# Hybrid attention, pooling, Fourier and mixture-of-experts backbone: branch projections as three products of split weights, and an opening in another order

## The chip, the cores and the metric

The kernel runs on one core of a Trainium2 chip. The metric is the device time of one execution in microseconds (us). Inputs are rearranged on the host beforehand and do not count.

## What is computed

Two layers run over 512 tokens of width 1024: 256 context tokens and 256 latent ones. The last layer needs context tokens as keys and values alone. Cut to what matters here:

```
for layer in range(2):
    h = rmsnorm(x, g_norm1) * (1 + scale1) + shift1       # shift, scale: c @ w_mod + b_mod
    p = h @ w_in                                           # q, kv, rope, pool, fourier, 3 gates
    a = attention(p)    # 8 heads, keys of context and latent tokens
    b = pooling(p)      # 4 window sizes, then a 128x128 product per group, times s_pool
    c = fourier(p)      # 2-D, per group of 128 channels
    g = sigmoid(p_gates + b_gate)
    y = g[0] * (a @ w_oa) + g[1] * (b @ w_ob) + g[2] * (c @ w_oc)    # branch projections
    x = x + gate1 * (y @ w_out)
    h = rmsnorm(x, g_norm2) * (1 + scale2) + shift2
    x = x + gate2 * (swiglu(h) if layer == 0 else top-2-of-8 experts(h))
return rmsnorm(x, g_final)
```

Everything is float32. Most products are made in a reduced format from two parts: a weight w is split into hi (w in the reduced format, fp32r) and lo (w - hi), the activations likewise, and hi*hi + hi*lo + lo*hi are added up.

## The kernel before

Channels lie on the 128 partitions, tokens along the free dimension: x is xT[128, 8, 512]. The order on each engine is written out by hand, with semaphores between engines. Layer 0 works on 512 columns, layer 1 (but for keys and values) on the 256 latent ones.

**The stream of split weights.** The dense weights come as one stream of 128x128 blocks. `Walk` numbers them in the order in which TensorE (PE) uses them, and cuts them into units of SPLIT_BLOCKS = 16 blocks, 1 MB. SyncE (SP) loads a unit into `stage` (3 slots), ScalarE (ACT) makes its high part (`split_hi`, line 675, whi), VectorE (DVE) the low part (`split_lo`, line 1040, wlo; 2 slots), and `block_passes` (lines 1605 to 1607) makes three products of each block. A high part waits until PE has walked over the unit two before, a load until the low part three before is made.

**Branch projections.** `branch(m)` (line 1838) makes a tile of 128 output channels of one branch: four plain f32 products of a block in `dw` with the branch's rows in `br`. Each f32 product shows in the trace as two matmuls. The blocks come through a second stream, `direct` (512 KB a unit, 3 slots), which also holds the pool product's weights, `v`, and the heads. There are 24 such tiles a layer, in the order of MERGE; PE makes the gate of tile m (`gate_half` twice, 8 blocks of the split stream), then the branch. All branches go to PSUM bank 1 and all gates to bank 0. So branch(m) waits for o_used, which the first DVE operation of `merge(m-1)` gives (yacc at line 1269 or gm at line 1276). The tiles 0 to 15 are made beside attention, the last eight (BESIDE on) after it.

**Attention.** An item is one head and 128 queries: 32 items in layer 0, 16 in layer 1. PE makes for item n the scores (line 1789), every so often queries and keys of the next head (lines 1748, 1756), then half a gate in layer 0 or a whole gate and its branch in layer 1 (`halves`), then turns item n-1 (1800) and multiplies item n-2 with the values (1813). DVE finds the row maximum (1241, 1243), turns positions of the next head's queries (1228 to 1235), merges, normalises (1249, 1251), and then makes a low part. ACT makes the exponential (835), copies queries and keys (809, 817), a high part, and the gate's tanh (855). A head's output goes to `br` in one copy (1260).

**The opening.** SP loads in order: the condition, its rows (`gw`), the eight small constants, x, four units of modulation weights for DVE (`mw_b`), four for PE (`mw_a`), then four and four again. ACT squares x (line 695) in two slots, PE sums the squares with `ones` (`first_squares`, line 1639), DVE makes modulation tiles (`mod_units`, 1145) and the root. PE makes rows of modulation (`early_rows`, 1624), ACT copies them (755), PE turns them (`early_turn`, 1631), and spreads the norm (`everywhere`, 1659). In a norm DVE makes nt (1088), ACT two scalings per tile, one per stream (729, hf), and the high part (720), and DVE the low part (1080), on which the first product (1605) waits.

**The pool joint.** After the Fourier tiles (1708, 1718; DVE copies each to `br`, 1218) come four pool products (1735); ACT copies each, scaled (803).

## Time and profile before

| | us |
|---|---|
| median of 3 runs | 2039.86 |
| lowest, highest | 2038.47, 2040.59 |
| the profiled execution | 2039.14 |
| its span, first to last instruction | 2037.4 |
| mean granted clock | 0.978 |
| busy: PE, PE weight loads | 1963.6, 1553.9 |
| busy: DVE, ACT, GpSimd (POOL) | 1364.3, 990.8, 91.0 |

The span is one profiled execution. Busy times are sums over instructions; matmuls overlap and their ends are modelled, so PE's pace is better read from the starts of successive groups. Idle time of an engine costs nothing unless PE waits for it. By the trace the opening lasts until 51.5, layer 0 until 896, layer 1's mixer until 1186, the experts until about 2010.

### The profile page before, as it was taken

How to read it: one execution, taken by the hardware profiler on the slowest of the kernel's cores; microseconds unless marked ns; L12 is line 12 of the kernel's file. 1: busy time of each engine (PE TensorE's matmuls, PEld its weight loads, DVE VectorE, ACT ScalarE, POOL GpSimd, SP SyncE). 2: the span in 40 equal slices, each digit the busy share in tenths (PEclk: the TensorE clock that was granted, in tenths of full speed). 3: DMA queues.
4: the chain of work that ended last, by engine and by line, in shares of the span. 5: the costliest groups of instructions: out<-in, count | busy, mean ns of one | idle time of the engine just before them, and what ended most of it. 6: DMA issues, size and time to landing. Idle time of an engine off the chain costs nothing.

```text
span 2037.4 us, 24090 instructions
## 1 busy us (share of the span) xinstructions
PE 1963.6 (96%) x9008; PEld 1553.9 (76%) x9008; DVE 1364.3 (67%) x1590; ACT 990.8 (49%) x1098; POOL 91.0 (4%) x127
## 2 busy tenths in 40 slices
PE   6999999999899999989999989999999999999997
PEld 3785666667688888868788978888878887888886
DVE  5753444377567646455344568888888888888995
ACT  3423333222522122243434367777767776777774
POOL 0150000000000001002000000000000000000000
PEclk9999999999899999989999979999999999999997
DMA  9312112244255556413233279989988998899980
GB/s 366 127 69 83 42 73 88 88 166 163 96 175 185 187 184 231 176 63 134 83 120 150 94 310 355 355 345 352 347 317 345 352 346 318 345 353 345 355 309 23
DMA packets 72401, 438.76 MB, mean 215 GB/s; under 512 B 9184, under 2 KB 9952, under 8 KB 28000
## 3 DMA queue, kind: packets, MB, share of 16 engines
q1 hardware_dynamic: 60624, 394.18, 51.1%
q0 software_dynamic: 11664, 43.00, 6.0%
q8 instruction: 80, 1.31, 0.2%
q14 instruction: 33, 0.27, 0.0%
HBM read 436.09 MB, written 1.05 MB: 215 GB/s over the span
## 4 chain that ended last, share of the span: by engine, by line
PE 92%; DVE 3%; ACT 2%; issue 2%; DMA 0%; SPq 0%; ACTq 0%; DVEq 0%
PE ps L1605 12%; PE ps L1606 12%; PE ps L1607 12%; PE ps L1993 8%; PE ps L1994 8%; PE ps L1995 8%; PE ps L1838 6%; PE ps L2007 4%; PE ps L2011 4%; PE ps L2008 4%; PE ps L1789 2%; PE ps L1813 2%; PE ps L1748 2%; PE ps L1639 1%; PE ps L1718 1%
## 5 line engine op out<-in xcount | busy, mean ns | idle before, releaser
L1422 DVE TENSOR_TENSOR elo<-estage,ehi 128x2048 fp32r<-128x2048 f32 x264 | 604.9, 2292 | 82.9 <-ACT ehi L933 81.7
L933 ACT ACTIVATE ehi<-estage 128x2048 fp32r<-128x2048 f32 x264 | 505.2, 1914 | 51.3 <-PE ps L2011 47.1
L1605 PE MATMUL ps<-h_hi,whi 128*128 128x512 f32 (+1 forms) x960 | 370.7, 386 | 17.7 <-DVE h_lo L1080 8.8
L1606 PE MATMUL ps<-h_lo,whi 128*128 128x512 f32 (+1 forms) x960 | 347.6, 362 | 0.0
L1607 PE MATMUL ps<-h_hi,wlo 128*128 128x512 f32 (+1 forms) x960 | 347.4, 362 | 0.0
L1993 PE MATMUL ps<-ehi,xg_hi 128*128 128x512 f32 x704 | 288.5, 410 | 8.2 <-issue 3.0
L1994 PE MATMUL ps<-elo,xg_hi 128*128 128x512 f32 x704 | 279.5, 397 | 0.0
L1995 PE MATMUL ps<-ehi,xg_lo 128*128 128x512 f32 x704 | 279.2, 397 | 0.0
L1040 DVE TENSOR_TENSOR wlo<-stage,whi 128x2048 fp32r<-128x2048 f32 x79 | 181.2, 2295 | 98.2 <-ACT whi L675 98.1
L675 ACT ACTIVATE whi<-stage 128x2048 fp32r<-128x2048 f32 x79 | 150.8, 1909 | 164.7 <-PE ps L1607 163.9
L1605 PEld LDWEIGHTS ps<-h_hi,whi 128*128 128x128 f32 x960 | 184.0, 192 | 59.3 <-issue 20.7
L1606 PEld LDWEIGHTS ps<-h_lo,whi 128*128 128x128 f32 x960 | 184.3, 192 | 36.3 <-issue 10.3
L1607 PEld LDWEIGHTS ps<-h_hi,wlo 128*128 128x128 f32 x960 | 183.8, 191 | 27.7
L1993 PEld LDWEIGHTS ps<-ehi,xg_hi 128*128 128x128 f32 x704 | 133.4, 189 | 36.0 <-issue 3.5
L1995 PEld LDWEIGHTS ps<-ehi,xg_lo 128*128 128x128 f32 x704 | 133.3, 189 | 32.4
L1994 PEld LDWEIGHTS ps<-elo,xg_hi 128*128 128x128 f32 x704 | 133.8, 190 | 27.4
L2007 PE MATMUL ps<-ehi,ehT_hi 128*128 128x512 f32 x352 | 137.8, 392 | 2.7 <-DVE ehT_lo L1440 2.6
L2008 PE MATMUL ps<-elo,ehT_hi 128*128 128x512 f32 x352 | 137.1, 389 | 0.0
L1838 PE MATMUL ps<-br,dw 128*128 128x512 f32 (+1 forms) x384 | 131.6, 485 | 0.0
L1145 DVE SCALAR_TENSOR_TENSOR gw<-gw,crow 128x1024 f32<-128x1024 f32 x80 | 98.3, 1238 | 21.0 <-DMA gw<-in_mods 21.0
L2011 PE MATMUL ps<-ehi,ehT_lo 128*128 128x512 f32 x352 | 108.9, 390 | 0.0
L1838 PEld LDWEIGHTS ps<-br,dw 128*128 128x128 f32 x384 | 71.0, 189 | 40.2 <-issue 34.5
(224 smaller groups left out, 2375.8 us busy)
## 6 DMA issues: line engine op xcount, KB each, us to landing
estage<-in_moe SPq DMA_DIRECT2D x264, 1024.0 KB, 5.0
stage<-in_split SPq DMA_DIRECT2D x79, 1024.0 KB, 4.9
gw<-in_mods POOLq DMA_DIRECT2D x80, 512.0 KB, 3.8
dw<-in_direct SPq DMA_DIRECT2D x36, 512.0 KB, 3.6
mw_b<-in_mods SPq DMA_DIRECT2D x8, 512.0 KB, 12.6
mw_a<-in_early SPq DMA_DIRECT2D x8, 512.0 KB, 14.3
xT<-in_x SPq DMA_DIRECT2D x1, 2048.0 KB, 7.9
gw<-in_cond_rows SPq DMA_DIRECT2D x1, 1024.0 KB, 5.0
```

The costliest lines, as they stand in the source:

```text
L933: act.activation(ehi[:, w % SPLIT, :], estage[:, w % STAGE, :], ACT.Copy).then_inc(S("e_hi_done"), 1)
L1422: dve.tensor_tensor(elo[:, w % SPLIT, :], estage[:, w % STAGE, :], ehi[:, w % SPLIT, :], ALU.subtract)\
L1605: pe.matmul(out, hi, rhs_hi, start=first, stop=False)
L1606: pe.matmul(out, hi, rhs_lo, start=False, stop=False)
L1607: ins = pe.matmul(out, lo, rhs_hi, start=False, stop=last)
L1838: ins = pe.matmul(ps[1][:, 0:T - lc], dw[:, slot, 4 * (m % 2) + k, :], br[:, b, k, lc:T], start=(k == 0), stop=(k == KB - 1))
L1993: pe.matmul(o, xg_hi[:, x % 2, kk, :], hi[:, cols], start=(kk == 0), stop=False)
L1994: pe.matmul(o, xg_hi[:, x % 2, kk, :], lo[:, cols], start=False, stop=False)
L1995: ins = pe.matmul(o, xg_lo[:, x % 2, kk, :], hi[:, cols], start=False, stop=(kk == KD - 1))
L2007: pe.matmul(ps[3 + f][:, :], a_hi, hi[:, cols], start=first, stop=False)
L2008: pe.matmul(ps[3 + f][:, :], a_hi, lo[:, cols], start=False, stop=False)
L2011: ins = pe.matmul(ps[3 + f][:, :], a_lo, hi[:, cols], start=False, stop=last)
```

## The change

1. **Units of 8 blocks** (512 KB) with 3 slots for the parts instead of 16 blocks with 2. `ahead` and `unit_of` say how far ahead parts are made. Beside attention and in the merges after it, the call of the parts stands before `merge` on DVE, and directly after the exponential and copies on ACT.
2. **Branch projections from the split stream**: after each gate's eight blocks follow its branch's four, and `branch` calls `block_passes`. The branch's rows are therefore kept in two parts, br_hi and br_lo: one more DVE operation for a Fourier tile, a pool group and a head's output, and two more for a head that is copied to the other partitions.
3. **The pool product's weights** have a place of their own (pw). The direct stream keeps `v` and the heads (10 units, 2 slots).
4. **The opening**: loads in another order, with semaphores for two loads each; all eight squares are kept and GpSimd adds them up; PE starts with the modulation rows.
5. **Shared scaling**: in three norms DVE makes the second stream's scaling of every other tile (`second_half`).

```diff
-SPLIT_BLOCKS = 16
+SPLIT_BLOCKS = 8
-DIRECT = 3
+DIRECT = 2
-DENSE_SPLIT = 2
+DENSE_SPLIT = 3
...
-        tiles += [(("gate", layer, m), KD) for m in range(KD * BRANCHES)]
+        for m in range(NM):
+            tiles += [(("gate", layer, m), KD), (("proj", layer, m), KB)]
...
+    def unit_of(self, key, k):
+        return self.block(key, k) // SPLIT_BLOCKS
+    def ahead(self, *key):
+        return self.units_up_to(*key) + DENSE_SPLIT - 1
...
-        load_small(*small[0]).then_inc(S("consts"), 16)
...
-        for t, a in small[1:]:
+        load_start_mods(0)
+        for t, a in small[:2]:
             load_small(t, a).then_inc(S("consts"), 16)
+        load_early_mods(0)
         sp.dma_start(xT[:, :, :], A["x"]).then_inc(S("x_in"), 16)
-        load_start_mods(0)
-        load_early_mods(0)
         load_start_mods(1)
+        for t, a in small[2:]:
+            load_small(t, a).then_inc(S("consts"), 16)
         load_early_mods(1)
...
+                turned_rows(0)
                 for k in range(KD):
                     square("n1_0", 0, k)
+                split_hi(1)
                 root("n1_0", 0)
...
+                turned_rows(1)
+                split_hi(2)
...
                     for m, half in halves(layer, n):
+                        split_hi(walk.unit_of(("gate", layer, m), KD // 2 * half) + DENSE_SPLIT)
                         if half == 1:
                             gate_tanh(m)
...
                     if n % per == 0 and todo[n][0] + 1 < HEADS:
                         head_rope(todo[n][0] + 1)
+                    for m, half in halves(layer, n):
+                        split_lo(walk.unit_of(("gate", layer, m), KD // 2 * half) + DENSE_SPLIT)
                 if 1 <= n <= len(todo):
                     for m, half in halves(layer, n - 1):
                         if half == 1:
...
             def after_merge(m):
-                split_lo(walk.units_up_to("gate", layer, m) + 1)
...
+                for k in range(1, KD):
+                    pool.wait_ge(S("norm_sq"), k + 1)
+                    if k >= 2:
+                        pool.wait_ge(S("start_add"), k - 1)
+                    pool.tensor_tensor(sq_ends[:, 0, :], sq_ends[:, 0, :], sq_ends[:, k, :], ALU.add).then_inc(S("start_add"), 1)
...
         pe.wait_ge(S("cond"), 2)
         pe.wait_ge(S("consts"), 16 * EARLY_CONSTS)
-        first_squares()
-        early_rows(0)
-        early_rows(1)
+        early_rows(0, 0, KD)
         early_turn(0)
+        early_rows(1, 0, KD - 2)
+        start_squares()
+        early_rows(1, KD - 2, KD)
+        early_turn(1)
         everywhere("n1_0", 0)
-        early_turn(1)
...
                 for k in range(KB):
-                    ins = pe.matmul(ps[1][:, 0:T - lc], dw[:, slot, 4 * (m % 2) + k, :], br[:, b, k, lc:T], start=(k == 0), stop=(k == KB - 1))
-                ins.then_inc(S("o_full"), 1)
+                    block_passes(ps[1][:, 0:T - lc], ("proj", layer, m), k, br_hi[:, b, k, lc:T], br_lo[:, b, k, lc:T], k == 0, k == KB - 1)
```

Three places of the order. First DVE in layer 1's attention, two items, the first with queries and the second without, before (L1241 row maximum, L1276 and L1269 the first operation of a merge, L1040 a low part):

```order
L1241 TENSOR_REDUCE stat<-ps 128x1 [waits s_full]
L1243 TENSOR_SCALAR stat<-stat 128x1 [waits max]
L1228 TENSOR_TENSOR qT<-ps,rope 32x256 [waits qk_full]
...
L1276 SCALAR_TENSOR_TENSOR gm<-gate,ps 128x256 [waits y_add,gate,o_full]
L1279 TENSOR_TENSOR yacc<-yacc,gm 128x256 [waits o_used]
...
L1241 TENSOR_REDUCE stat<-ps 128x1 [waits s_full]
L1243 TENSOR_SCALAR stat<-stat 128x1 [waits max]
L1269 SCALAR_TENSOR_TENSOR yacc<-gate,ps 128x256 [waits gate,o_full]
L1249 RECIPROCAL stat<-stat 128x1 [waits prob]
L1251 TENSOR_SCALAR prob<-prob,stat 128x512 [waits rden]
L1040 TENSOR_TENSOR wlo<-stage,whi 128x2048 [waits hi_done]
```

and now (L1282 row maximum, L1327 and L1320 the merge, L1061 a low part of half the size):

```order
L1282 TENSOR_REDUCE stat<-ps 128x1 [waits s_full]
L1284 TENSOR_SCALAR stat<-stat 128x1 [waits max]
L1269 TENSOR_TENSOR qT<-ps,rope 32x256 [waits qk_full]
...
L1061 TENSOR_TENSOR wlo<-stage,whi 128x1024 [waits hi_done]
L1327 SCALAR_TENSOR_TENSOR gm<-gate,ps 128x256 [waits y_add,gate,walked]
...
L1282 TENSOR_REDUCE stat<-ps 128x1 [waits s_full]
L1284 TENSOR_SCALAR stat<-stat 128x1 [waits max]
L1061 TENSOR_TENSOR wlo<-stage,whi 128x1024 [waits hi_done] x2
L1320 SCALAR_TENSOR_TENSOR yacc<-gate,ps 128x256 [waits gate,walked]
L1290 RECIPROCAL stat<-stat 128x1 [waits prob]
```

The low parts have moved from behind the merge and the normalisation to in front of them: one in the items with an even number, two in the others.

SP at the start of the program, before:

```order
L593 DMA gw<-in_cond_rows 128x2048
L590 DMA ones<-in_ones 128x128
...
L590 DMA g_kv<-in_g_kv 128x4
L608 DMA xT<-in_x 128x4096
L604 DMA mw_b<-in_mods 128x1024 x4
L599 DMA mw_a<-in_early 128x1024 x4
L604 DMA mw_b<-in_mods 128x1024 x4
L599 DMA mw_a<-in_early 128x1024 x4
```

and now:

```order
L604 DMA gw<-in_cond_rows 128x2048
L614 DMA mw_b<-in_mods 128x1024 x4
L601 DMA ones<-in_ones 128x128
L601 DMA ident<-in_ident 128x128
L609 DMA mw_a<-in_early 128x1024 x4
L620 DMA xT<-in_x 128x4096
L614 DMA mw_b<-in_mods 128x1024 x4
L601 DMA b_mod<-in_b_mod 128x96
...
L601 DMA g_kv<-in_g_kv 128x4
L609 DMA mw_a<-in_early 128x1024 x4
```

Six of the eight constants have moved from the front to behind x and the second four mw_b loads, and x from the front to behind four loads of each kind.

PE's opening now, where before the squares of x came first, with the same wait for the constants (L1685 modulation rows, L1693 the turn, L1701 squares, L1720 the spread of the norm):

```order
L1685 MATMUL ps<-mw_a,cond_t 2x512 [waits early_in0,consts,cond]
L1685 MATMUL ps<-mw_a,cond_t 2x512 x3
L1685 MATMUL ps<-mw_a,cond_t 2x512 [waits early_in1]
...
L1693 MATMUL ps<-ident,m_rows 128x2 [waits m_rows]
...
L1685 MATMUL ps<-mw_a,cond_t 2x512 [waits early_in3]
...
L1701 MATMUL ps<-ones,sq_ends 128x1 [waits start_add]
L1701 MATMUL ps<-ones,sq_ends 128x1 x3
L1685 MATMUL ps<-mw_a,cond_t 2x512 x2
...
L1720 MATMUL ps<-diag,ones 128x512 [waits norm_diag]
```

The squares have moved behind the first group of rows and most of the second, and four summing products are left of 32.

## Rows read from the trace of the kernel before

**Rows 1.** The page, chain that ended last, share of the span by engine.

```profile
PE 92%; DVE 3%; ACT 2%; issue 2%; DMA 0%; SPq 0%; ACTq 0%; DVEq 0%
```

**Rows 2.** The chain in order of time, branch products: start us, us, what.

```profile
407.07 3.43 PE ps L1838 x8
...
469.28 3.45 PE ps L1838 x8
...
1121.56 1.73 PE ps L1838 x8
...
1153.76 1.74 PE ps L1838 x8
```

**Rows 3.** Timeline, layer 1's attention, item without queries: start us, us, engine, line.

```profile
1029.05 1.13 PE L1789 MATMUL ps<-kT,qT 96*128 96x512 f32 x2
...
1031.02 0.42 DVE L1269 SCALAR_TENSOR_TENSOR yacc<-gate,ps 128x256 f32<-128x256 f32 x1
...
1031.71 0.19 ACT L835 ACTIVATION_READ_ACCUMULATOR prob<-ps,stat 128x1 f32 x1
...
1032.89 0.59 PE L1838 MATMUL ps<-br,dw 128*128 128x256 f32 x2
```

**Rows 4.** Timeline, the next item, with queries.

```profile
1036.17 1.12 PE L1789 MATMUL ps<-kT,qT 128*128 128x512 f32 x2
...
1039.18 1.90 ACT L675 ACTIVATE whi<-stage 128x2048 fp32r<-128x2048 f32 x1
...
1041.30 1.03 PE L1838 MATMUL ps<-br,dw 128*128 128x256 f32 x4
```

**Rows 5.** Groups by form: busy us, mean ns of one, idle before.

```profile
L1040 DVE TENSOR_TENSOR wlo<-stage,whi 128x2048 fp32r<-128x2048 f32 x79 | 181.2, 2295 | 98.2 <-ACT whi L675 98.1
L1080 DVE TENSOR_TENSOR h_lo<-hf,h_hi 128x512 fp32r<-128x512 f32 x24 | 16.3, 691 | 8.1 <-ACT h_hi L720 8.1
L720 ACT ACTIVATE h_hi<-hf 128x512 fp32r<-128x512 f32 x24 | 14.5, 615 | 0.0
```

**Rows 6.** The opening: timeline, a load's time to landing, and DMA rate (last column).

```profile
27.91 15.99 PE L1624 MATMUL ps<-mw_a,cond_t 128*2 128x512 f32 x32
34.18 1.24 POOL L1540 DMA_DIRECT2D gw<-in_mods  x2 [33.72 <-DMA mw_a<-in_early]
37.07 0.59 ACT L755 ACTIVATE m_rows<-ps 2x512 f32<-2x512 f32 x1 [8.51 <-PE ps L1624]
43.94 0.59 ACT L755 ACTIVATE m_rows<-ps 2x512 f32<-2x512 f32 x1 [2.04 <-PE ps L1624]
47.39 1.28 DVE L1088 TENSOR_TENSOR nt<-xT,ps 128x512 f32<-128x512 f32 x2
51.54 0.79 PE L1605 MATMUL ps<-h_hi,whi 128*128 128x512 f32 x1 [4.62 <-DVE h_lo L1080]
router<-in_router SPq DMA_DIRECT2D x1, 32.0 KB, 18.2
26.00:30.00 4.00, 4.00 (x13) 2.23 (x13) 3.69 (x11) 0.74 (x2) 0.00 (x0) 1.00 1.03 410
```

**Rows 7.** Timeline of GpSimd: an add alone, and one beside two low parts.

```profile
126.11 1.09 POOL L1573 TENSOR_TENSOR win<-pool_in 128x542 f32<-128x542 f32 x1
...
955.98 4.85 POOL L1582 TENSOR_TENSOR br<-win,pool_in 128x256 f32<-128x256 f32 x1 [2.54 <-DVE pq L1205]
```

**Rows 8.** A wait of PE after layer 0's merges, and the window behind it (clock third from last).

```profile
479.95 0.79 PE L1605 MATMUL ps<-ym_hi,whi 128*128 128x512 f32 x1 [3.15 <-DVE ym_lo L1311]
...
480.00:484.00 4.00, 4.00 (x10) 3.13 (x11) 3.78 (x5) 0.17 (x1) 0.12 (x1) 0.50 0.51 145
```

**Rows 9.** Scalings, the pool joint, and DVE (third figure pair) in layer 0's merges.

```profile
901.18 2.07 ACT L729 ACTIVATE hf<-nt,mod,coef 128x256 f32<-128x256 f32 x4 [3.66 <-DVE nt L1088]
...
156.44 3.92 PE L1735 MATMUL ps<-br,dw 128*128 128x512 f32 x8 [0.61 <-DVE br L1218]
...
440.00:472.00 32.00, 32.00 (x115) 21.42 (x114) 23.60 (x34) 6.62 (x9) 3.17 (x6) 1.00 0.43 153
```

More of the change, by code:

```diff
@@ L208, in direct_stream @@
     for layer in range(DEPTH):
-        out += [("pool", layer), ("v", layer), ("head", layer, 0)]
-        for h in range(HEADS):
-            if h % 2 == 1 and h + 1 < HEADS:
-                out.append(("head", layer, (h + 1) // 2))
-            out.append(("proj", layer, h))
-        out += [("proj", layer, n) for n in range(HEADS, NM // 2)]
+        out += [("v", layer)] + [("head", layer, c) for c in range(HEADS // 2)]
     return out
@@ L267, in load_order @@
             tile("in", layer, j)
-        for m in range(2 * DENSE_SPLIT):
-            tile("gate", layer, m)
-        for key in [("pool", layer), ("v", layer), ("head", layer, 0)]:
-            add(("d", direct_at[key]))
-        for m in range(KD * BRANCHES):
+            if j == 4:
+                add(("p", layer))
+            if j == 8:
+                add(("d", direct_at[("v", layer)]))
+                add(("d", direct_at[("head", layer, 0)]))
+        for m in range(NM):
             tile("gate", layer, m)
@@ L276, in load_order @@
                 add(("d", direct_at[("head", layer, m // 4 + 1)]))
-            add(("d", direct_at[("proj", layer, m // 2)]))
+            tile("proj", layer, m)
         for j in range(KD):
@@ L286, in load_order @@
                     tile("down", half, j)
-    assert len(out) == walk.units + len(direct_at)
+    assert len(out) == walk.units + len(direct_at) + DEPTH
     return out
@@ L491, in direct_used @@
         kind, layer, *rest = direct[n]
-        if kind == "pool":
-            return S("pool_full"), earlier("pool_full", layer) + GROUPS
         if kind == "v":
             return S("v_full"), earlier("v_full", layer) + T // P
-        if kind == "head":
-            return S("qk_full"), qk_full(layer, "q", 2 * rest[0] + 1)
-        return S("o_full"), earlier("o_full", layer) + 2 * (rest[0] + 1)
+        return S("qk_full"), qk_full(layer, "q", 2 * rest[0] + 1)
     def c0(layer):
@@ L556, in nth, with shared, scaled @@
         return [t for t, _ in norms].index(tag)
+    def shared(tag, k):
+        return k % 2 == 1 and tag in ("n1_0", "n2_0", "n1_1")
+    def scaled(tag, k):
+        per = KD * 3 // 2
+        return per * nth(tag) + (k + 1 if tag == "n2_1" else 2 * (k + 1) - (k + 1) // 2)
     def summed(tag):
-        return KD + nth(tag)
+        return 1 + nth(tag)
     def added(tag, k):
@@ L846, in gate_tanh @@
             def gate_tanh(m):
-                split_hi(walk.units_up_to("gate", layer, m) + 1)
                 j, b = MERGE[m]
@@ L881, in _ @@
             for m in range(BESIDE, NM):
+                for half in (0, 1):
+                    split_hi(walk.unit_of(("gate", layer, m), KD // 2 * half) + DENSE_SPLIT)
                 gate_tanh(m)
@@ L888, in _ @@
             for j in range(KD):
-                split_hi(walk.units_up_to("out", layer, j) + 1)
+                split_hi(walk.ahead("out", layer, j))
                 square(f"n2_{layer}", lc, j)
@@ L1167, in _ @@
         coefs(0, 0)
+        split_lo(2)
         for layer in range(DEPTH):
@@ L1172, in _ @@
             for j, name in enumerate(TILES):
-                split_lo(walk.units_up_to("in", layer, j) + 1)
+                split_lo(walk.ahead("in", layer, j))
                 if name == "kr":
@@ L1314, in _ @@
             for m in range(BESIDE, NM):
+                for half in (0, 1):
+                    split_lo(walk.unit_of(("gate", layer, m), KD // 2 * half) + DENSE_SPLIT)
                 merge(m)
@@ L1321, in _ @@
             for j in range(KD):
-                split_lo(walk.units_up_to("out", layer, j) + 1)
+                split_lo(walk.ahead("out", layer, j))
                 if j >= 2:
@@ L1358, in _ @@
                     for j in range(KD):
-                        split_lo(walk.units_up_to("down", half, j) + 1)
+                        split_lo(walk.ahead("down", half, j))
                         if half == 1 and j >= 2:
@@ L1726, in _ @@
                 tokens(n)
-            slot = direct_unit(("pool", layer))
+            pe.wait_ge(S("pool_in"), 16 * (layer + 1))
             for g in range(GROUPS):
@@ L1733, in _ @@
                 else:
-                    pe.wait_ge(S("br_b"), earlier("br_b", layer) + g - 1)
-                pe.matmul(ps[4 + g % 2][:, 0:T - lc], dw[:, slot, g, :], mixed[:, 0, g, lc:T], start=True, stop=True)\
+                    pe.wait_ge(S("br_b_lo"), earlier("br_b_lo", layer) + g - 1)
+                pe.matmul(ps[4 + g % 2][:, 0:T - lc], pw[:, g, :], mixed[:, g, lc:T], start=True, stop=True)\
                     .then_inc(S("pool_full"), 1)
@@ L1795, in turn @@
                 if n < 2:
-                    pe.wait_ge(S("br_b"), earlier("br_b", layer) + GROUPS)
+                    pe.wait_ge(S("br_b_lo"), earlier("br_b_lo", layer) + GROUPS)
                 else:
@@ L2206, in layout @@
         unit = np.zeros((P, DIRECT_BLOCKS, P), np.float32)
-        if kind == "pool":
-            unit[:, 0:GROUPS] = i["w_pool"][layer].transpose(1, 0, 2)
-        elif kind == "v":
+        if kind == "v":
             v = i["w_ukv"][layer][:, :, NOPE:].reshape(KKV, P, HEADS * VD)
```

150 lines of the change are left out of this document (89 added, 61 removed).

## Prediction

> **What bounds the kernel now.** I read the chain of waits first. TensorE (PE) carries 92% of it and no other engine over 3% [rows 1]: a matmul that becomes cheaper is worth its full price, and work on another engine costs nothing until PE waits for it. Then, in the same chain, the pace of the part that is rewritten. Without attention beside it, the loop over output tiles in layer 0 begins its branch products (line 1838) at 407.07 and, seven tiles on, at 469.28: 8.89 us a tile, 3.43 of them the branch and 5.46 the 24 products of the gate, 0.227 each. In layer 1 (256 columns) the tile takes 4.60, the branch 1.73, a gate product 0.120 [rows 2]. PE does not wait in either stretch. Last the timelines: one attention item of layer 1 engine by engine [rows 3, 4], and the opening [rows 6].
>
> **The branch products.** Before, four f32 blocks, two passes each, cost 3.43 and 1.73 us a tile. Now each block is three products of the gate's kind: 12 x 0.227 = 2.73 and 12 x 0.120 = 1.44. Saved: 24 x 0.70 = 16.8 us in layer 0 and 24 x 0.29 = 7.1 in layer 1, together 23.9, as long as PE stays the bound. The Trainium skill (FP8 and Floating Point Precision, TensorE Precision Notes) counts a true FP32 product as four passes. Three for four would save a quarter of the branch time, 31 us; the rows give a fifth, and I go by the rows.
>
> **The split halves move ahead of the merge.** This is the term I find decisive. The rows of the order show it: in layer 1 VectorE (DVE) now makes one or two low parts (wlo) between the row maximum and the merge; before, it made one after both. PE's branch(m) waits for the first operation of merge(m-1), since all branches share one PSUM bank. Take an item without queries (n odd), counted from the start of its score products [rows 3]. ScalarE's exponential and its sum are done at +2.85, the merge starts at +1.97, and PE reaches the branch at +3.85. Now ScalarE makes two high parts from +2.75. A 128x1024 copy lies between the 128x512 copy and the 128x2048 one [rows 5, 4]: 0.61 and 1.90 give 1.04. DVE's low part likewise: 0.69 and 2.29 give 1.22 [rows 5]. First high part at +3.8, second at +4.7 (its buffer comes free in the middle of the gate, before that), low parts at +5.0 and +6.2, merge's first operation (0.42) at +6.55. PE waits until then: 2.7 us. The eight odd items: 21.6 us; three of them also make keys, which shifts both sides about equally.
>
> In an item with queries (n even) one part is due. ScalarE begins it at +3.0, where the whole one began [rows 4]; high part +4.05, low +5.3, merge +5.7; PE is at the branch at +5.1: 0.6 us, in seven items 4. Where an odd head was finished, DVE has two more operations of 0.42 at the item's head: 0.5 in three items. The last even item has no queries and waits another 1. The sum is 28; what may overlap I take off, **26 us**. The bounds: 0, if the merge is never late, and 50, below. Layer 0 is safe: there a tile takes two items, and the merge ahead of the branch runs in the first of them, a whole item early. After attention the merge comes before the next tile's parts, and in layer 0, where DVE was busy 23.6 of 32 us [rows 9], 6.6 a tile, one and a half low parts of 1.22 for half a one of 2.29 make it 7.2 of the new tile's 8.2: no wait yet, and the cover nearly used up. Gone, each tile would cost what DVE is over.
>
> **The opening.** PE now begins with the early modulation rows, but its first wait still asks for all eight small constants, and six of them are issued behind x and the second four mw_b loads. Transfers of this queue land in order: router, 32 KB, took 18.2 us. The last mw_a load landed at 34.2 behind some 11,500 KB [rows 6]; the last small constant now has some 9,450 KB ahead, 2 MB less, and at 410 GB/s that is 5.1 us earlier: 29.1. The 16 products of the first row group took from 27.9 to 37.1, 9.1 us [rows 6]; now until 38.2. ScalarE's copy of them (0.6) stands ahead of the squares of x, so the squares begin at 38.9, though x has long landed. Two squares, 0.6 each, then GpSimd's seven adds: 1.09 is the row of a 542-wide add alone [rows 7], 1.17 with the handover, 8.2. While DVE wrote two low parts, one short add took 4.85 [rows 7], so DVE's first low part (1.22) puts them off by 1.1: 49.4. The summing products 1.7, the last products of the second row group 2.4, so 53.5. From its copy (43.94) to the first scaling (47.39) it was 3.45; the norm's spread no longer stands before the turn (-1.1), one low part does (+1.2): 57.1. The first real product was 4.15 us behind (51.54) and is now 3.65 behind: 60.8. That is **9.3 us later**, between -4.5 (no constant late: the adds hidden behind the loads, and the squares off PE) and +13 (products at half pace after the idle).
>
> **Small terms.** Shared scaling: the first h_hi stood behind four scalings, 2.07 us [rows 9], now behind three. In the norms of n2_0 and n1_1 -0.5 each, **-1.0**; the rest of a norm is paced by PE. At the joint of Fourier and pool the last fourier tile needs a second DVE operation before the pool product, which already waits 0.61 [rows 9]; each later pair of pool products waits for a low part: 0.45 and 0.7 in layer 0, 0.4 and 0.45 in layer 1, **+2.0**. Head outputs, now two or three operations each, in layer 0 hide under the item's gate half; that cover gone, 1.4 a head. Loads of 512 KB for 1,024 KB: three units of layer 1 last 8.6 us of PE, and the loads there are not near it. The reciprocals of layer 1's norm still hold up one low part; I leave that at 0 (-1 to +2). The experts do not change.
>
> **The sum.** Profiled execution 2039.1 (span 2037.4, 1.7 around it), 0.7 below the median of the runs: 2039.1 - 23.9 + 26 + 9.3 + 2.0 - 1.0 = 2051.5.
>
> **The rivals.**
> *The stalls cost the clock too.* After PE's idle of 3.15 us the granted clock was 0.50, the lower level of 1.2 GHz, over the next 4 us and not at once back [rows 8]; that cost about 3 us. A wait of 2.7 is a little shorter. If each of the eight does the same, 24 more: 2075. Against it: the idle is shorter than any that the row shows. 15%. The Trainium skill (TensorE: Matmul & The Clock Gate, Why this matters for your kernels) warns that idle gaps between bursts of matmuls bring the half rate back; no row here shows where that begins for gaps this short.
> *The merge isn't late.* This is the one that ends faster. Place: DVE in layer 1's attention. If the high parts are made an item earlier than I read, because the buffer is long free and ScalarE gets to them before the exponential, DVE has both low parts done by +3.4 and the wait is gone. It decides at +3.85 less 0.42. Then 2051.5 - 26 = 2025.5; 13%. Against it stands the order, row maximum, wlo, wlo, merge, on an engine that takes its work in order.
> *Neither stall, and the constants are not late:* 2025.5 - 13.8 = 2011.7. It asks that small loads overtake large ones, which router's 18.2 speaks against. 7%.
> *Late merges, timely constants:* 2051.5 - 13.8 = 2037.7, no change. 9%.
> *The forecast:* 2044 to 2061 (the stall sum 20 to 32, the opening 7 to 12). 56%.
>
> **How the numbers follow.** The likeliest case gives 2051.5. The range takes in the clock case and the one without stalls, and leaves out the 7% below and the upper part of the clock case: 2023 to 2074. 0.2%, 4 us, is about what a measurement of this kernel can tell from no change. Faster by more: 13 + 7 and a little of the rest, 0.21. Within: the 9 and the low tail of the forecast, 0.11. Slower: 0.68.
>
> **What would show it.** In the changed profile: branch products of layer 0 that take 2.73 a tile after attention, with periods of 8.2 and 4.3; PE waits for the merge operation (DVE, yacc or gm) in layer 1, about fifteen of them, 2.7 and 0.6 long by turns; in layer 0's attention none. The granted clock in these items 1.00, or near 0.6 if the clock rival holds. In the opening the first PE product near 29, squares of x near 39, seven GpSimd adds until 49, the first product with h_hi near 61. An odd item of layer 1, 7.12 us before from score to score [rows 3, 4], should take 9.5; if it takes 6.8, the stall term is wrong; if the first h_hi product comes before 51, the opening is.

## The result, and the profile after

| | before | after |
|---|---|---|
| median of 4 runs, us | 2039.59 | 2070.80 |
| lowest, highest | 2038.47, 2040.59 | 2070.07, 2072.87 |
| profiled execution, span | 2037.4 | 2071.1 |
| mean granted clock | 0.978 | 0.969 |

The ratio is 1.0155, 95% interval 1.0137 to 1.0172: the change makes the kernel 31 us slower. I had forecast 12 us slower. The profiled execution of the changed kernel is the slowest of its four, so the two spans differ by 33.7.

Where it went, by the starts of the first product of each stage in the two profiled executions (us; the last column is what my sum had):

| stage | before | after | difference | forecast |
|---|---|---|---|---|
| opening | 51.54 | 64.80 | +13.3 | +9.3 |
| projections in, layer 0 | 83.32 | 83.05 | -0.3 | |
| Fourier, pool, v, layer 0 | 37.34 | 38.58 | +1.2 | +1.1 |
| attention and merges, layer 0 | 299.95 | 288.14 | -11.8 | -16.8 |
| projection out, layer 0 | 50.25 | 48.21 | -2.0 | |
| norms n2_0, n1_1 | 20.89 | 20.53 | -0.4 | -1.0 |
| feed-forward, layer 0 | 361.26 | 360.70 | -0.6 | |
| projections in, layer 1 | 62.01 | 61.32 | -0.7 | |
| Fourier, pool, v, layer 1 | 24.21 | 25.19 | +1.0 | +0.9 |
| attention and merges, layer 1 | 164.36 | 198.54 | +34.2 | +18.9 |
| projection out, router, experts | 865.36 | 865.52 | +0.2 | |
| final norm and output | 16.88 | 16.51 | -0.4 | |

The shape is the forecast one; three stages lie 4, 5 and 15 us above it. The waits of PE say most of it (`<-` names what ended the wait). First the whole program (us in total, times, longest):

```profile
PE ps L1685 <- DMA g_kv<-in_g_kv: 29.0, 1, 29.0
PE ps L1665 <- DVE yacc L1320: 19.7, 8, 2.6
...
PE ps L1665 <- DVE gm L1327: 6.1, 7, 1.6
...
PE ps L1701 <- POOL sq_ends L1606: 5.4, 1, 5.4
```

and layer 0 from the first scores to the end of the merges alone:

```profile
PE ps L1665 <- DVE wlo L1061: 3.3, 1, 3.3
```

Fifteen waits for the merge, 25.8 us, against 26 in the sum; the first one of PE ends at 29.0, against 29.1. The 3.3 was not in the sum.

The item of layer 1 without queries, the answer to [rows 3] (timeline: start us, us, engine, line):

```profile
1037.69 1.12 PE L1851 MATMUL ps<-kT,qT 96*128 96x512 f32 x2
...
1038.85 0.69 DVE L1282 TENSOR_REDUCE stat<-ps 128x1 f32<-128x512 f32 x1 [3.24 <-PE ps L1851]
...
1041.53 2.36 DVE L1061 TENSOR_TENSOR wlo<-stage,whi 128x1024 fp32r<-128x1024 f32 x2 [1.79 <-ACT whi L691]
...
1043.81 0.41 DVE L1320 SCALAR_TENSOR_TENSOR yacc<-gate,ps 128x256 f32<-128x256 f32 x1
1044.28 0.38 PE L1665 MATMUL ps<-br_hi,whi 128*128 128x256 f32 x1 [2.60 <-DVE yacc L1320]
...
1044.62 0.28 PE L1667 MATMUL ps<-br_hi,wlo 128*128 128x256 f32 x1
...
1045.58 0.42 PE L1667 MATMUL ps<-br_hi,wlo 128*128 128x256 f32 x1
...
1048.91 0.70 PE L1851 MATMUL ps<-kT,qT 128*128 128x512 f32 x1
```

The two low parts stand between the row maximum and the merge; the merge's first operation ends at +6.53 (forecast +6.55), and PE waits 2.60. Then comes what I had given 15%: behind the wait the products take 0.28 us for less than a microsecond and 0.42 from then on. The item is 11.22 long, where it was 7.12 before; I had said 9.5. The granted clock in windows of the same stretch (the third figure from the end; 0.50 is 1.2 GHz, 1.00 is 2.4):

```profile
1041.70:1044.28 2.58, 0.00 (x1) 0.01 (x1) 2.58 (x4) 0.74 (x1) 0.00 (x0) 1.00 0.12 22
1044.28:1046.30 2.02, 2.02 (x12) 2.02 (x13) 0.50 (x2) 0.47 (x1) 0.00 (x0) 0.68 0.92 310
1046.30:1047.60 1.30, 1.30 (x7) 0.97 (x7) 0.00 (x0) 0.07 (x1) 0.00 (x0) 0.50 0.70 274
```

Full clock during the idle, the lower level behind it. So it is in seven of the eight odd items. In the fourth of them the wait is 2.25 us and the window behind it reads

```profile
1065.96:1068.00 2.04, 2.04 (x16) 1.90 (x16) 0.50 (x2) 0.47 (x1) 0.00 (x0) 1.00 0.92 347
```

with no lower level at all. The Trainium skill (TensorE: Matmul & The Clock Gate, Why this matters for your kernels) warns of idle gaps between bursts of matmuls, but of longer ones than these; this trace shows the drop at a gap of 2.60, and the measurement decides.

The opening after, the answer to [rows 6]:

```profile
28.96 9.84 PE L1685 MATMUL ps<-mw_a,cond_t 128*2 128x512 f32 x16 [28.96 <-DMA g_kv<-in_g_kv]
...
39.34 4.25 ACT L708 ACTIVATE sq_ends<-xT 128x512 f32<-128x512 f32 x8
40.55 10.58 POOL L1606 TENSOR_TENSOR sq_ends<-sq_ends 128x512 f32<-128x512 f32 x7 [40.09 <-ACT sq_ends L708]
51.18 1.86 PE L1701 MATMUL ps<-ones,sq_ends 128*128 128x1 f32 x8 [5.41 <-POOL sq_ends L1606]
52.98 3.57 PE L1685 MATMUL ps<-mw_a,cond_t 128*2 128x512 f32 x4
57.23 1.86 PE L1693 MATMUL ps<-ident,m_rows 2*128 2x2 f32 x8 [0.68 <-ACT m_rows L768]
59.02 2.08 PE L1720 MATMUL ps<-diag,ones 128*128 128x512 f32 x2
61.13 1.28 DVE L1120 TENSOR_TENSOR nt<-xT,ps 128x512 f32<-128x512 f32 x2 [0.35 <-PE ps L1720]
64.80 0.79 PE L1665 MATMUL ps<-h_hi,whi 128*128 128x512 f32 x1 [3.71 <-DVE h_lo L1101]
```

The chain is the forecast one, constants, rows, copy, squares, adds, with most links somewhat longer. The place of the first h_hi product moves from one execution to the next: in the four runs below that leave the opening and its norm as they are (merge_first, fill, one_behind, beside) it came at 63.75, 63.79, 64.38 and 61.80. The idle of 5.41 is there in all of them; the lower clock behind it lasted some 7 us in beside and 17 to 20 in the others. So the opening costs 10.3 to 13.3 us, and this execution shows the upper end.

Last the pace of the rewritten branch behind attention, the first branch product of two tiles in a row, layer 0 and layer 1:

```profile
439.21 0.39 PE L1665 MATMUL ps<-br_hi,whi 128*128 128x512 f32 x1
...
447.37 0.39 PE L1665 MATMUL ps<-br_hi,whi 128*128 128x512 f32 x1
...
1161.70 0.28 PE L1665 MATMUL ps<-br_hi,whi 128*128 128x256 f32 x1
...
1166.02 0.28 PE L1665 MATMUL ps<-br_hi,whi 128*128 128x256 f32 x1
```

8.16 and 4.32 a tile, against 8.89 and 4.60 [rows 2] and a forecast of 8.2 and 4.3.

### The profile page after: what moved, and what is told of

It is laid out like the page before. It is cut to its first block, busy times and chain, and to the rows that moved or that the text cites. A ratio compares the mean times of both kernels' runs of the same rounds, so it can differ in the third digit from the quotient of the medians.

```text
span 2071.1 us, 24850 instructions
## 1 busy us (share of the span) xinstructions
PE 1946.2 (94%) x9144; PEld 1569.3 (76%) x9144; DVE 1427.3 (69%) x1749; ACT 1019.4 (49%) x1189; POOL 99.0 (5%) x134
## 3 DMA queue, kind: packets, MB, share of 16 engines
HBM read 435.57 MB, written 1.05 MB: 211 GB/s over the span
## 4 chain that ended last, share of the span: by engine, by line
PE 69%; DVE 4%; ACT 3%; issue 3%; ACTq 0%; DVEq 0%
PE ps L1665 9%; PE ps L1667 9%; PE ps L1666 9%; PE ps L2053 8%; PE ps L2054 7%; PE ps L2055 7%; PE ps L2067 4%; PE ps L2071 4%; PE ps L2068 4%; DVE wlo L1061 1%; ACT whi L691 1%; PE ps L1875 1%; PE ps L2039 1%; ACT ehi L954 1%; PE ps L1851 1%
## 5 line engine op out<-in xcount | busy, mean ns | idle before, releaser
L1061 DVE TENSOR_TENSOR wlo<-stage,whi 128x1024 fp32r<-128x1024 f32 x182 | 223.9, 1239 | 166.6 <-ACT whi L691 166.4
L691 ACT ACTIVATE whi<-stage 128x1024 fp32r<-128x1024 f32 x182 | 190.8, 1054 | 259.1 <-PE ps L1667 258.7
L1665 PE MATMUL ps<-br_hi,whi 128*128 128x512 f32 (+1 forms) x192 | 68.5, 357 | 25.8 <-DVE yacc L1320 19.7
L978 ACT ACTIVATE ehT_hi<-ps 128x256 fp32r<-128x256 f32 x88 | 33.8, 384 | 117.5 <-PE ps L2039 117.5
```

What stands on the lines that cost most here:

```text
L691: act.activation(whi[:, u % DENSE_SPLIT, :, :], stage[:, u % DENSE_STAGE, :].rearrange("p (b c) -> p b c", c=P), ACT.Copy)\
L1061: dve.tensor_tensor(wlo[:, u % DENSE_SPLIT, :, :], stage[:, u % DENSE_STAGE, :].rearrange("p (b c) -> p b c", c=P), whi[:, u % DENSE_SPLIT ...
L1665: pe.matmul(out, hi, rhs_hi, start=first, stop=False)
```

## The experiments

Every ratio is to the kernel before, run beside it on the same chip; its median there was 2039.78 to 2039.90 us (2038.59 in the single run beside combined_again). Differences to the changed kernel are to its 2070.80. In the diffs, lines are of the changed kernel unless said otherwise.

**merge_first: the low parts behind the merge, in attention.**

```diff
                     row_max(n)
...
-                    for m, half in halves(layer, n):
-                        split_lo(walk.unit_of(("gate", layer, m), KD // 2 * half) + DENSE_SPLIT)
...
                     normalise(n)
+                    for m, half in halves(layer, n):
+                        split_lo(walk.unit_of(("gate", layer, m), KD // 2 * half) + DENSE_SPLIT)
```

> The changed kernel with one thing moved on DVE, in the attention loops of both layers: the low parts are made behind the merge and the normalisation, as before the change, instead of ahead of them. Theory A (the late merge costs its waits and, in the odd items of layer 1, the lower clock behind them): the waits of PE for yacc and gm, 19.7 + 6.1 = 25.8 us, go, and with them the time lost to the lower level, about 12 us: 2070.8 - 38 = 2033, and the stretch of layer 1's attention and merges falls from 198.5 to about 161. Theory B (the waits alone): 2045. Rival C (the twelve us come from somewhere else, such as the larger number of blocks in the stream): the waits go and the stretch stays above 170.

Measured: 2029.45 us, ratio 0.9946 (0.9929 to 0.9962), 41 below the changed kernel. Attention and merges of layer 1 take 158.15. The waits for the merge are gone; the item without queries (timeline; scores, merge, low parts):

```profile
1025.51 1.12 PE L1851 MATMUL ps<-kT,qT 96*128 96x512 f32 x2
...
1027.47 0.42 DVE L1320 SCALAR_TENSOR_TENSOR yacc<-gate,ps 128x256 f32<-128x256 f32 x1
...
1029.35 2.36 DVE L1061 TENSOR_TENSOR wlo<-stage,whi 128x1024 fp32r<-128x1024 f32 x2 [0.27 <-ACT whi L691]
```

The merge starts at +1.96 again and the item lasts 6.82, the old 7.12 less the cheaper branch. So the order of two calls on DVE cost 198.54 - 158.15 = 40.4 us: 25.8 of waits and 14.6 behind them. Theory A; B is out by 16, and C, that something else costs the rest, is out too.

**fill: PE kept busy in the waits.** Does it take the idle to lower the clock?

```diff
+                    if layer == 1 and m % 2 == 1 and m < BESIDE:
+                        for _ in range(20):
+                            ins = pe.matmul(ps[0][:, SEQ:T], h_hi[:, 0, 0:P], h_hi[:, 1, lc:T], start=True, stop=True)
+                        ins.then_inc(S("filled"), 1)
                     pe.wait_ge(S("o_used"), earlier("o_used", layer) + m)
...
+                if layer == 1 and m % 2 == 1 and m < BESIDE:
+                    act.wait_ge(S("filled"), (m + 1) // 2)
```

> The changed kernel with 20 products of 256 columns added ahead of PE's wait for the merge, in the eight odd items of layer 1's attention. They write columns of bank 0 that nobody reads, and ScalarE's tanh of the gate waits for them. They take 20 x 0.12 = 2.4 us, in a wait that lasts 2.25 to 2.60 us, so PE does useless work where it stood idle and the merge comes no earlier. Theory A (the idle lowers the clock behind it): the branch, the turns and the values behind it run at full clock, and the time falls by 8 x 1.5 = 12 us, to 2059. Theory D (the clock falls for another reason, or the slow products have nothing to do with it): no gain, 2071 to 2073.

Measured: 2060.07 us, ratio 1.0094 (1.0077 to 1.0111): 10.7 us faster than the changed kernel, by doing 160 useless products more. The long waits of PE in layer 1's attention, now 0.9 in all, and two windows of it (busy of PE first, clock third from the end):

```profile
PE ps L1667 <- DVE yacc L1322: 0.9, 5, 0.2
```

```profile
1016.00:1024.00 8.00, 8.00 (x65) 7.55 (x64) 3.25 (x5) 4.40 (x8) 0.00 (x0) 1.00 0.33 113
1024.00:1032.00 8.00, 7.18 (x49) 6.17 (x48) 5.55 (x12) 3.12 (x6) 0.00 (x0) 1.00 0.26 93
```

The clock is 1.00 in both; in the changed kernel it was 0.79 from 1024 to 1032. The item without queries lasts 9.66 instead of 11.22. The fourth odd item, the one whose wait no lower clock followed, lasts 11.04 in both kernels. That is the direct test: the merge comes no earlier, PE is only not idle, and 10.9 us of the stretch go. Of the 14.6 behind the waits, 3.7 stay. They are not the clock. An even item lasts 9.19: 8.12 of merge_first, 0.82 of wait, and 0.25 more. The starts in the trace account for it. A wait is counted from the end of the last product's record, which lasts 0.28 while the products start every 0.12 (0.16), and the first product behind the wait is followed after 0.22 and not 0.12 (0.10). Fifteen waits at 0.25 are the 3.7; the items of one_behind and before_low show the same 0.25.

**one_behind: one of the two low parts behind the merge.**

```diff
                     for m, half in halves(layer, n):
+                        if layer == 1 and half == 1:
+                            continue
                         split_lo(walk.unit_of(("gate", layer, m), KD // 2 * half) + DENSE_SPLIT)
...
                     normalise(n)
+                    if layer == 1:
+                        for m, half in halves(layer, n)[1:]:
+                            split_lo(walk.unit_of(("gate", layer, m), KD // 2 * half) + DENSE_SPLIT)
```

> The changed kernel, with only the low part of each item's second gate half moved behind the normalisation, in layer 1's attention. Items that made two low parts ahead of the merge now make one. The long waits (2.25 to 2.60 us, eight of them) should fall by one low part, 1.2 us, to about 1.05 to 1.4; the short ones stay. That is 9 to 10 us. Theory A1 (the clock falls only behind a long idle; behind the one wait of 1.64 us it stayed at 1.00): the clock loss of about 12 us goes too, 2049. Theory A2 (each us of idle costs its share of clock): half of the twelve stays, 2055. If the items that are left with one low part now wait more, the sum is higher: 2058 or more.

Measured: 2049.79 us, ratio 1.0043 (1.0026 to 1.0060). The long waits, and a window with one of them:

```profile
PE ps L1670 <- DVE yacc L1320: 10.6, 8, 1.5
```

```profile
1000.00:1008.00 8.00, 6.55 (x45) 5.71 (x44) 5.51 (x11) 4.23 (x8) 0.00 (x0) 1.00 0.41 132
```

Waits of 1.3 in the mean leave the clock at 1.00, and 9.1 us less of waiting made 21 us less of time. A1 as it stood: the price of a wait here is not in proportion. In this stretch of the program the clock stayed at 1.00 behind every wait up to 1.64 us and fell behind seven of eight between 2.24 and 2.60; between 1.64 and 2.24 no run has a wait here.

**before_low: the same delay in the kernel before** (lines of that kernel).

```diff
                         if half == 1:
+                            if layer == 1:
+                                split_lo(walk.units_up_to("gate", layer, m) + 1)
                             merge(m)
```

> The kernel before, with its low part (2.29 us) moved ahead of the merge in layer 1's attention, and nothing else. In the odd items the merge's first operation then ends about 2.3 us later, at +4.7 from the score instead of +2.4, and PE is at the branch at +3.85: it waits 0.8 us in each of eight items, 6 to 7 us in all, and at idles this short the clock stays at 1.00: 2039.6 + 6.6 = 2046. If an idle of 0.8 also costs clock: 2050 to 2058. If the order on DVE does not matter: 2040.

Measured: 2043.64 us, ratio 1.0018 (1.0008 to 1.0027). One row:

```profile
PE ps L1840 <- DVE yacc L1269: 3.6, 5, 0.7
```

Slower, by 3.9 us and not 6.6: five items waited, about 0.7 each, and grew by 0.95. The order alone does it, without any other part of the change, and without loss of clock.

**beside: the low parts ahead of the modulation tiles, behind attention in layer 0.** The wait of 3.3 us is of PE for a low part at 424. What stood on DVE there, in the changed kernel:

```profile
413.93 2.29 DVE L1159 SCALAR_TENSOR_TENSOR crow<-crow,gw 128x2048 f32<-128x2048 f32 x1
...
420.36 1.23 DVE L1178 SCALAR_TENSOR_TENSOR junk_gate<-gw,crow 128x1024 f32<-128x1024 f32 x1 [4.14 <-issue]
...
422.66 2.35 DVE L1061 TENSOR_TENSOR wlo<-stage,whi 128x1024 fp32r<-128x1024 f32 x2
424.02 0.76 PE L1665 MATMUL ps<-h_hi,whi 128*128 128x512 f32 x1 [3.30 <-DVE wlo L1061]
```

DVE idles 4.14 us for modulation weights that GpSimd could only start to load when `crow` was made, and the low parts are queued behind. In the kernel before it idled 4.13 us at the same place, but had split 16 blocks ahead.

```diff
                     cond_rows(2)
+                    for half in (0, 1):
+                        split_lo(walk.unit_of(("gate", layer, m + 1), KD // 2 * half) + DENSE_SPLIT)
                 mod_units("gate", layer, m)
```

> The changed kernel with the low parts for the tile after the first one behind attention (layer 0) made ahead of the modulation tiles on DVE, which wait there 4.14 us for their loads. Theory: PE's wait of 3.30 us for a low part at 424 goes, and the lower clock of some 4 us behind it (1.5 to 2 us): 2070.8 - 5 = 2066, and attention and merges of layer 0 last 283 instead of 288. Rival (the wait only moves to a later tile, since DVE is as busy as PE in these tiles): 2069 to 2071.

Measured: 2065.50 us, ratio 1.0130 (1.0113 to 1.0147). Attention and merges of layer 0 take 283.10, and PE waits nowhere in the merges:

```profile
416.00:424.00 8.00, 8.00 (x37) 6.64 (x36) 6.24 (x11) 2.11 (x4) 1.00 (x2) 1.00 0.74 288
424.00:432.00 8.00, 8.00 (x37) 6.64 (x36) 7.97 (x14) 3.06 (x5) 0.84 (x3) 1.00 0.63 198
```

299.95 - 283.10 = 16.85 is the branch products' saving in layer 0, forecast as 16.8.

**opening_undone: the opening of before in the changed kernel.**

```diff
-        load_start_mods(0)
-        for t, a in small[:2]:
+        for t, a in small:
             load_small(t, a).then_inc(S("consts"), 16)
-        load_early_mods(0)
         sp.dma_start(xT[:, :, :], A["x"]).then_inc(S("x_in"), 16)
+        load_start_mods(0)
+        load_early_mods(0)
         load_start_mods(1)
-        for t, a in small[2:]:
-            load_small(t, a).then_inc(S("consts"), 16)
...
+        start_squares()
         early_rows(0, 0, KD)
+        early_rows(1, 0, KD)
...
```

(PE sums all eight squares, ScalarE squares first, GpSimd adds nothing.)

> The changed kernel with the opening of before: its order of loads, the squares of x first on ScalarE, all eight summed by PE (32 products), no adds on GpSimd, then the rows. The other four parts stay. Expected: the first h_hi product at 51.5 instead of 64.8, as in the kernel before, and everything behind it shifted by that: 2070.8 - 13.3 = 2057.5. If the time falls by less than 10, part of the opening's cost is paid back later in the changed kernel, and the term is smaller than the shift of the first product says.

Measured: 2059.97 us, ratio 1.0097 (1.0081 to 1.0114), the first h_hi product at 53.03 instead of 64.80. Of the 11.8 us there, 10.8 arrive in the time. The 1.5 to the 51.54 of before are mostly one low part (1.22) that stayed ahead of the norm.

**consts_front: only the six constants back in front.**

```diff
-        for t, a in small[:2]:
+        for t, a in small:
             load_small(t, a).then_inc(S("consts"), 16)
...
-        for t, a in small[2:]:
-            load_small(t, a).then_inc(S("consts"), 16)
```

> The changed kernel with the six small constants that it loads behind x and the second four mw_b loads put back in front of the mw_a loads; nothing else. Theory A (the wait for g_kv, 29.0 us, starts the whole chain of the opening late): PE begins near 14 to 17, when its first mw_a loads are in, the rows of the first group end near 25, the squares follow at once, GpSimd's seven adds (1.41 each) are done near 37, and the last mw_a load, near 34, becomes the bound: the first h_hi product near 51 instead of 64.8, 2057. Theory B (GpSimd's adds alone make it late, whenever they begin): the first h_hi product stays above 58, 2064 or more.

Measured: 2061.75 us, ratio 1.0106 (1.0089 to 1.0123), the first h_hi product at 55.89, 5 us later than I expected. The rows:

```profile
15.58 9.88 PE L1683 MATMUL ps<-mw_a,cond_t 128*2 128x512 f32 x16 [15.58 <-DMA mw_a<-in_early]
27.20 15.01 POOL L1604 TENSOR_TENSOR sq_ends<-sq_ends 128x512 f32<-128x512 f32 x7 [26.75 <-ACT sq_ends L706]
30.00 2.27 DVE L1176 SCALAR_TENSOR_TENSOR mw_b<-mw_b,crow 128x1024 f32<-128x1024 f32 x1
42.27 1.87 PE L1699 MATMUL ps<-ones,sq_ends 128*128 128x1 f32 x8 [4.17 <-POOL sq_ends L1604]
```

PE starts at 15.6, as A has it. But GpSimd's seven adds take 15.01 us instead of 10.58, and DVE's products beside them 2.1 to 2.3 instead of 1.22. So A is half right: between these two executions the late constants cost 8.9 us of the 13.3, and the adds become the bound behind them.

**adds_alone: DVE waits until GpSimd has added.**

```diff
         mod_units("start", 0)
+        dve.wait_ge(S("start_add"), KD - 1)
         mod_units("start", 1)
```

> The kernel of the run consts_front with one wait added: DVE begins its second four modulation tiles only when GpSimd's seven adds of squares are done. In consts_front both ran at once: the seven adds took 15.01 us, and DVE's products of 128x1024 took 2.1 to 2.3 us each instead of 1.22. Theory P (GpSimd and DVE hold each other up): alone, the adds take 10 us (1.41 each, handover included) from 27.2 on, though the loads still land until 34, and DVE's products behind them 1.22 each; they end near 48 instead of 42, and the first h_hi product comes between 52 and 54. Theory L (the landing loads slow both): the adds still take 12 us or more, since seven of them start before 36, and the first h_hi product comes later than 55.9.

Measured: 2064.27 us, ratio 1.0123 (1.0106 to 1.0140), the first h_hi product at 55.27. Rows:

```profile
25.86 9.71 POOL L1605 TENSOR_TENSOR sq_ends<-sq_ends 128x512 f32<-128x512 f32 x7 [25.41 <-ACT sq_ends L706]
30.33 8.13 PE L1684 MATMUL ps<-mw_a,cond_t 128*2 128x512 f32 x12 [4.48 <-DMA mw_a<-in_early]
36.76 1.22 DVE L1176 SCALAR_TENSOR_TENSOR mw_b<-mw_b,crow 128x1024 f32<-128x1024 f32 x1
47.69 1.86 PE L1692 MATMUL ps<-ident,m_rows 2*128 2x2 f32 x8 [6.44 <-ACT m_rows L766]
```

Alone, the adds take 9.71 and the products 1.22, while the loads still land: theory P, not L. The gain is used up by DVE, which now does its tiles later; the first product came 1.3 later than the upper end that I gave, behind a PE that had idled 6.44 and turned the second rows in 1.86, at the lower clock, where the kernel before took 1.05. As a remedy it is none.

**shared_off: the fifth part undone.**

```diff
     def shared(tag, k):
-        return k % 2 == 1 and tag in ("n1_0", "n2_0", "n1_1")
+        return False
...
```

(Behind it the counts of the scalings that other engines wait for are set back.)

> The changed kernel without its fifth part: ScalarE makes both streams' scalings of every tile again, DVE none. By my sum the part was worth 1.0 us in the norms of n2_0 and n1_1, and something in the first norm: 2070.8 + 1 to 2 = 2072.3, with the stretches of these norms longer by 0.3 to 0.5 each. If the part costs time (DVE is the fuller engine there), 2069 to 2070. Smaller than what the time of a run can tell; the stretches of the trace decide.

Measured: 2073.82 us, ratio 1.0169 (1.0152 to 1.0186), with a span 1.0 longer. The norms n2_0 and n1_1 take 10.78 and 10.68 instead of 10.29 and 10.24: the part is worth 0.5 and 0.4 us, as forecast (0.5 each). The projections behind the first norm take 84.00 instead of 83.05, but they vary by as much between kernels that share this norm (82.60 in fill, 83.97 in combined). The rest of the 3 us by the medians is not resolved.

**combined: all four repairs** (merge_first, beside, consts_front, and ScalarE's squares ahead of its copy of the rows).

```diff
-                turned_rows(0)
                 for k in range(KD):
                     square("n1_0", 0, k)
+                turned_rows(0)
...
```

> All repairs at once on the changed kernel: low parts behind the merge in attention, the constants in front, ScalarE's squares ahead of its copy of the rows, the low parts ahead of the modulation tiles behind attention. If the terms add up: 2029.5 (low parts behind the merge) - 14 (opening) - 5 (behind attention) = 2010, which is what the forecast gave for neither stall and timely constants (2011.7). If the opening is bound by the last mw_a load: 2013. If the repairs get in each other's way: 2020 or more.

Measured: 2014.02 us, ratio 0.9874 (0.9857 to 0.9890). It is 25.9 us faster than the kernel before and 56.8 faster than the change as it was made. The first h_hi product comes at 49.22. Forecast 2010; 4 us are given back, most of them in the stretch that the next run shows.

**combined_old_opening: the same with the opening of before.**

> The changed kernel with the low parts behind the merge, the low parts ahead of the modulation tiles behind attention, and the opening of before. In the run combined, which has the new opening repaired instead, the first h_hi product came at 49.2; with the old opening it came at 53.0. If the opening's shift is carried through: 2014.0 + 3.8 = 2018. If the two are worth the same in the end: 2014.

Measured: 2013.21 us, ratio 0.9873 (0.9856 to 0.9889): the same, though its first h_hi product comes 3.0 later. The trace says where those 3 us went: 1.0 to the projections into layer 0 (83.97 in combined, 83.02 here), and 2.9 to the output projection of layer 0, which takes 49.49 in combined and 46.61 here. In both, PE idles 2.8 us ahead of its product with `ym_lo`. The windows with that idle and behind it, first of combined:

```profile
459.00:463.00 4.00, 1.20 (x4) 0.87 (x4) 4.00 (x7) 0.00 (x0) 1.05 (x2) 0.78 0.48 143
463.00:467.00 4.00, 4.00 (x11) 3.13 (x10) 2.71 (x6) 1.18 (x2) 0.00 (x0) 0.50 0.75 240
```

then of combined_old_opening:

```profile
461.00:465.00 4.00, 1.19 (x5) 0.86 (x5) 4.00 (x7) 0.00 (x0) 1.05 (x2) 1.00 0.44 141
465.00:469.00 4.00, 4.00 (x19) 3.33 (x18) 4.00 (x8) 1.58 (x2) 0.00 (x0) 1.00 0.78 235
```

The same idle, once with the lower clock behind it and once without.

**combined_again: is that chance?** The kernel of combined, unchanged.

> The kernel of the run combined once more, unchanged. In combined, PE's idle of 2.8 us ahead of the output projection of layer 0 was followed by 4 us at a granted clock of 0.50, and that stretch took 49.49 us; in combined_old_opening the same idle was followed by 1.00, and the stretch took 46.61. Theory X (what an idle this short costs depends on when it falls, and differs from execution to execution): the stretch takes another value between 46.6 and 49.5, most likely not 49.5 again. Theory Y (it is fixed by the kernel): 49.5 again.

Measured, in a single execution: 2014.10 us, and 49.42 in that stretch. My theory X missed: it came out as before. Over all runs the stretch took 46.6, 48.2 or 49.4 us with the changed kernel's products (48.21 in the changed kernel, 46.66 in merge_first, where the stretch begins only 0.1 us earlier). The three values go with how long the lower clock lasted at the idle of 2.8: not at all, some 3 us, and some 7 us. What decides among these stays open. Shown is that the same products and the same idle can take 3 us more or less; that the shift of the program decides it is not shown.

## Why the prediction was wrong, by its own steps

The direction, the rivals and the mechanisms stood; the size did not (12 forecast, 31 measured). Step by step:

- **The branch products:** right. 16.85 in layer 0 once nothing waits (beside), and 6.2 in layer 1 (merge_first: 158.15 for 164.36) for a forecast of 7.1; 0.5 of the difference is a wait for the last head's low part, which I had left out. The decision for the rows (a fifth saved) against four passes (a quarter, 31 us) was right: 23 us.
- **The split halves ahead of the merge:** the waits right, 25.8 for 26, 2.24 to 2.60 in the eight odd items and 0.55 to 1.64 in the others. The mechanism held, but the last 2 us of the match are luck: the terms added up to 28, and what I took off for overlap had no row behind it.
- **What stands behind the stalls:** this is the step that failed most. The sum priced a stall at its own length and put the clock behind it at nothing; it stood beside the sum as a rival. I set its chance at 15% with the sentence "the idle is shorter than any that the row shows" and its price at 24. Waits of 2.24 to 2.60 were followed by the lower clock in seven of the eight odd items of layer 1's attention. The runs put its price at 10.9 (fill), and 3.7 more are the 0.25 that each wait costs beyond its counted length: 14.6 in all (merge_first), where the sum had 0. A wait only a sixth shorter than the one that the row shows to be costly belonged in the sum, at a part of that row's 3 us, and not beside it as a rival.
- **"Layer 0 is safe ... no wait yet, and the cover nearly used up":** wrong by 5.0. I compared DVE's mean busy time per tile [rows 9], and 7.2 of 8.2 fits. The wait of 3.3 comes from one instruction that stands for 4.14 us with the low parts queued behind it, where the part made ahead had shrunk from 16 to 8 blocks; the other 1.7 of the 5.0 go with the lower clock there. The mean over 32 us cannot show that; the timeline at 416 does, and the kernel before had the same idle.
- **The opening:** the step was mis-sized, 13.3 for 9.3, just beyond the bound of +13 (10.3 to 13.3 over the executions). The start was right (29.0 for 29.1). An add costs 1.27 and 0.14 of handover, not the 1.17 that I took from the row of a 542-wide one [rows 7]: 1.7 us over seven, less 0.3, since DVE's low part put them off by 0.8 and not 1.1. The rows took 0.7 longer. Behind the idle of 5.41 PE ran at the lower level: 3.57 for the last products (2.4 forecast), 1.86 for the turn of the rows, with the spread now behind it and not ahead. From the first scaling on, 3.67 for 3.65.
- **The pool joint** 2.2 for 2.0, **the norms** -0.4 in all for -1.0, of which the shared scaling is -0.9 (shared_off) and 0.5 is lost elsewhere in them.
- **The rest**, -3.8, was in no term: the output projection of layer 0 took 2.0 less (the lower clock at its first product lasted some 3 us, in the kernel before some 7), the feed-forward and the projections into layer 1 0.6 and 0.7, and smaller ones.

In the sum: -16.8 + 5.0 - 6.2 + 25.8 + 14.6 + 13.3 + 2.2 - 0.4 - 3.8 = 33.7, the difference of the two spans.

## What to carry to other kernels

A change that makes a matrix product cheaper is worth no more than the order of the small work around it: here 23 us were gained and 40 lost, because one or two operations of 1.2 us were put ahead of the one that PE waits for, and moving two lines back made the same change 10 us faster than the kernel before. Price a new wait of PE by its length and, as a range, by the clock behind it, and look for it instruction by instruction on an in-order engine, above all behind an operation that itself waits for a load: a mean busy share doesn't show it. Constants that many instructions wait for in one sum of a semaphore belong in front of the large loads, or each wait should ask only for those that it needs (this second remedy was not tried).

## What the runs showed of the hardware

- **Idles of 2.24 to 2.60 us were followed by a granted clock of 0.50 in seven cases of eight**, beginning between 0.1 us before and 1.1 us after PE resumed, for some 3 us. These items were 1.2 to 1.6 us longer than in fill, 10.9 for the stretch. Behind the eighth wait, 2.25 us at 1065.96, the clock stayed at 1.00, and so it did behind the same wait in beside, consts_front, adds_alone, opening_undone and shared_off.
- **The length of the idle alone does not decide.** In layer 1's attention no idle up to 1.64 was followed by the lower clock, but in the norm at 898.23 the clock fell behind idles of 0.84 and 1.61 in a row. At 2.8 us it fell in some kernels and not in others (combined, combined_old_opening). An idle of 3.45 in the experts of the changed kernel, at 1746.49, was followed by 1.00.
- **GpSimd and DVE hold each other up.** GpSimd's add of 128x512 took 1.26 alone and 2.06 beside DVE's products, which took 1.22 alone and 2.1 to 2.3 beside it. In consts_front it made the seven adds 4.4 us longer than in the changed kernel. The rows of the median add, alone (adds_alone) and beside (consts_front), ns min/median/max:

```profile
L1605 POOL TENSOR_TENSOR sq_ends<-sq_ends x7: 1259/1263/1269, 25.9 to 34.3; 128x512 f32<-128x512 f32 x7
```

```profile
L1604 POOL TENSOR_TENSOR sq_ends<-sq_ends x7: 1777/2058/2070, 27.2 to 40.2; 128x512 f32<-128x512 f32 x7
```

  The Trainium skill (SBUF — State Buffer, Who interferes with whom) states that the two share a pair of ports, which one instruction holds until it ends. The trace agrees: in the changed kernel a low part that DVE had begun at 44.57 took its usual 1.23, and the add issued beside it at 44.80 took 2.12 and ended 1.1 behind it. In consts_front the two engines alternate, one add and one product every 2.2 us.
